# Two output projections of a two-block transformer kernel, each as seven block products in place of eight

## The reference

```python
merged = sigmoid(a_r) * y_r + sigmoid(a_f) * y_f      # 1024 tokens x 1024, two gated heads' outputs
x = x + merged @ w_out[l]                             # the output projection, 1024 x 1024
h2 = rmsnorm(x, g_ffn[l])                             # block 1 goes on to its feed-forward
```

## Time and profile before

| | |
|---|---|
| time, median of 3 runs | 3076.11 us (3071.45 to 3077.84) |
| time of the profiled execution | 3070.67 us |
| its span | 3068.9 us |
| busy: PE, DVE, ACT, POOL | 96%, 49%, 34%, 31% |
| projection of block 1, first matmul to first of the feed-forward | 830.04 to 928.15 us |
| projection of block 2, first matmul to the end of the span | 2967.86 to 3068.9 us |
| matmuls of one projection | 384 |

### The profile page before, as it was taken

The page is one execution under the profiler, slowest core; times in us unless marked ns, Lnnn a source line. Parts: engine busy times, 40 slices in busy tenths (PEclk is TensorE's granted clock), DMA queues, the critical chain, the costliest instruction groups (busy, mean ns, idle before and its releaser), DMA issues.

```text
span 3068.9 us, 38355 instructions
## 1 busy us (share of the span) xinstructions
PE 2937.8 (96%) x14282; PEld 2348.7 (77%) x14282; DVE 1510.8 (49%) x2003; ACT 1038.5 (34%) x1732; POOL 942.6 (31%) x725
## 2 busy tenths in 40 slices
PE   7989999999998999999998999999999999999998
PEld 6778776788786888887887766668788888788886
DVE  2573656311317665653436488850556566651133
ACT  3232555300114333321223366641444444530011
POOL 2424110344442000003446600013333443444444
PEclk8999999999999999999999999999999999999999
DMA  3111000211224222224113300013323322241132
GB/s 127 42 47 55 18 28 18 93 48 45 75 82 141 83 83 83 83 90 185 47 48 125 101 7 14 21 37 103 86 71 81 82 74 79 73 158 48 44 110 86
DMA packets 107446, 224.13 MB, mean 73 GB/s; under 512 B 14001, under 2 KB 27057, under 8 KB 106801
## 3 DMA queue, kind: packets, MB, share of 16 engines
q1 hardware_dynamic: 67680, 134.01, 14.4%
q10 hardware_dynamic: 39632, 88.26, 8.4%
HBM read 167.70 MB, written 41.94 MB: 68 GB/s over the span
## 4 chain that ended last, share of the span: by engine, by line
PE 77%; DVE 11%; ACT 5%; issue 3%; POOL 2%; DMA 2%; ACTq 1%; POOLq 0%; SPq 0%; DVEq 0%
PE ps L356 17%; PE ps L372 13%; PE ps L2046 12%; PE ps L317 12%; PE ps L2166 7%; PE ps L1085 3%; PE ps L1116 1%; PE ps L2370 1%; DMA raw<-in_stream_dram 1%; DVE mla_ptl L1049 1%; ACT ps L1025 1%; PE ps L1101 1%; POOL wl L3373 1%; DVE mla_nm L1058 1%; PE ps L1103 1%
## 5 line engine op out<-in xcount | busy, mean ns | idle before, releaser
L3371 POOL TENSOR_TENSOR wh<-raw,zeros 128x512 fp32r<-128x512 f32 x356 | 397.9, 1118 | 2091.0 <-PE ps L372 559.7
L3373 POOL TENSOR_TENSOR wl<-raw,wh 128x512 fp32r<-128x512 f32 x356 | 531.5, 1493 | 27.9
L372 PE MATMUL ps<-hth,wh 128*128 128x512 f32 x704 | 285.0, 405 | 2.1 <-DVE fox_vl L1298 2.1
L372 PE MATMUL ps<-hth,wl 128*128 128x512 f32 x704 | 278.9, 396 | 0.0
L372 PE MATMUL ps<-htl,wh 128*128 128x512 f32 x704 | 278.7, 396 | 0.0
L317 PE MATMUL ps<-wh,hth 128*128 128x512 f32 (+2 forms) x608 | 237.3, 390 | 12.8 <-POOL wl L3373 7.7
L317 PE MATMUL ps<-wl,hth 128*128 128x512 f32 (+2 forms) x608 | 234.0, 385 | 0.0
L317 PE MATMUL ps<-wh,htl 128*128 128x512 f32 (+2 forms) x608 | 233.7, 384 | 0.0
L356 PE MATMUL ps<-hth,wh 128*128 128x512 f32 x496 | 196.6, 396 | 0.4 <-issue 0.3
L356 PE MATMUL ps<-hth,wl 128*128 128x512 f32 x496 | 196.3, 396 | 0.0
L356 PE MATMUL ps<-htl,wh 128*128 128x512 f32 x496 | 196.2, 395 | 0.0
(11 more groups left out here) (495 smaller groups left out, 6819.1 us busy)
## 6 DMA issues: line engine op xcount, KB each, us to landing
raw<-in_stream_dram SPq DMA_DIRECT2D x356, 256.0 KB, 2.6
up_raw<-in_stream_dram SPq DMA_DIRECT2D x21, 1024.0 KB, 5.7
dil_stg<-dil_stg ACTq DMA_DIRECT2D x96, 128.0 KB, 2.4
ff_dram<-ff SPq DMA_DIRECT2D x20, 512.0 KB, 3.0
dil_sz<-vd_dram ACTq DMA_DIRECT2D x12, 512.0 KB, 4.4
heads_raw<-heads_dram ACTq DMA_DIRECT2D x8, 512.0 KB, 7.2
norm_x<-in_x_dram ACTq DMA_DIRECT2D x1, 4096.0 KB, 16.1
x_dram<-norm_x ACTq DMA_DIRECT2D x8, 512.0 KB, 3.1
```

The lines of the kernel that those rows point to most:

```text
L372: ins = nc.tensor.matmul(ps[:, bank + half, :], w[:, j, c:c + P], a[:, k, HALF * half:HALF * half + HALF], start=k == 0 and q == 0, stop=k ...
L3371: nc.gpsimd.tensor_tensor(wh[:, s, :], raw[:, s, :], zeros[:].to_broadcast([P, HALF]), ALU.add).then_inc(w_hi, 1)
L3373: nc.gpsimd.tensor_tensor(wl[:, s, :], raw[:, s, :], wh[:, s, :], ALU.subtract).then_inc(w_split, 1)
```

## The change

`M` is cut in two by two blocks: P (features 0 to 511, tokens 0 to 511), Q (features 512 to 1023, the same tokens), and R and S for tokens 512 to 1023. The weights are cut in the same way into E, F (features 0 to 511; left and right output columns) and G, H (features 512 to 1023). The result's four blocks are made from seven block products, with sums of blocks as their operands: `pe` = P E, `qg` = Q G, `s1w1`, `s2w2`, `s4f`, `s3w3` and `rw4`, where S1 = R + S, S3 = Q - S, S2 = S1 - Q, S4 = P - S2, w1 = H - G, w2 = F - w1, w4 = E - w2, w3 = F - H. A block product is four weight units times four token tiles times 3 matmuls, 48 in all; the projection has 7 x 48 = 336 matmuls where it had 384.

- `pe`, `qg` and `s4f` take their weights from the stream (12 units for a projection, where there were 16), and each unit now serves four token tiles. The weights of the other four products are sums of blocks: ACT loads E, F, G, H again from a copy at the stream's end, DVE makes the sums, ACT their high parts `Wh`, DVE their low parts `Wl`.
- DVE makes the sums of blocks of `M` in place, and their low parts (`norm_ml`).
- `early_loads` and `early_sum` load H and G and make w1 at the start of the merge, in the second slot of the gates' tile `sg`; ACT's gates of column 1 wait for that (`early_summed`).
- Token tiles 0 to 3 are complete with the fifth product, `s4f`; their norm, and in block 1 the transposes of tiles 0 to 3, now lie within `s3w3` and `rw4`. The last product, `rw4`, is made token tile by token tile, 9 matmuls each.

```diff
-    plain(w["w_out"][0], range(KT))
+    def out_units(a):
+        for ks, c in ((K1, 0), (K2, 0), (K1, 1)):
+            for k in ks:
+                unit(rows(a, k, HALF * c, HALF))
+    out_units(w["w_out"][0])
...
-U_A, U_FOX, U_MERGE, U_OUT, U_UP, U_DOWN, U_LAT, U_MLA, U_DIL = 24, 28, 48, 16, 8, 44, 16, len(AHEAD) + 7, 80
+U_A, U_FOX, U_MERGE, U_OUT, U_UP, U_DOWN, U_LAT, U_MLA, U_DIL = 24, 28, 48, 12, 8, 44, 16, len(AHEAD) + 7, 80
...
+                if late:
+                    self.Wh = sb(name + "_wh", [P, 4, HALF], F32R, scope)
+                    self.Wl = sb(name + "_wl", [P, 4, HALF], F32R, scope)
+                    self.Ml = sb(name + "_ml", [P, KT, S], F32R, scope)
+                    self.S1h = sb(name + "_s1h", [P, 4, HALF], F32R, scope)
+                    with ExitStack() as over:
+                        self.E = sb(name + "_e", [P, 4, HALF], F32, over)
...
+            def early_loads(self, act):
+                act.dma_start(self.norm.F[:], self.weights(K2, 1)).then_inc(self.early_in, 16)
+                for br in range(2):
+                    act.dma_start(self.merge.sg[:, br, 1, :].rearrange("p (a n) -> p a n", a=2), self.weights(K2[2 * br:2 * br + 2], 0)).then_inc(self.early_in, 16)
+            def early_sum(self, dve):
+                dve.wait_ge(self.early_in, 48)
+                for br in range(2):
+                    at = self.norm.F[:, 2 * br:2 * br + 2, :]
+                    self.v.did(nc.vector.tensor_tensor(at, at, self.merge.sg[:, br, 1, :].rearrange("p (a n) -> p a n", a=2), ALU.subtract), "w1" + "ab"[br])
+            def early_summed(self, act):
+                self.v.wait(act, "w1b")
 
...
+                def copy(out, x, step):
+                    a.did(nc.scalar.activation(out, x, ACT.Copy), step)
+                def high(w, x, j, product):
+                    if product:
+                        p.wait(act, f"{product}.u{j}" if j < 3 else f"{product}.3")
+                    copy(n.Wh[:, j, :], x[:, j, :], f"h{w}.{j}")
...
+                m.py.wait(act, "y0", last)
+                act.dma_start(n.X[:, 0:4, :], self.source[:, 0:4, :]).then_inc(self.x_in[0], 16)
+                m.v.wait(act, "m1", last)
+                act.dma_start(n.E[:], self.weights(K1, 1)).then_inc(self.f_in, 16)
+                n.load(act)
+                m.v.wait(act, "sum", last)
+                copy(hth[:, last, 0:HALF], m.M[:, last, 0:HALF], f"hi{last}")
+                for j in range(4):
+                    high("w1", n.F, j, None)
+                v.wait(act, "s1b")
+                copy(n.S1h[:], self.R, "s1h")
...
+                v.wait(dve, "s3b")
+                tt(self.Q, self.R, self.Q, "s2")
+                a.wait(dve, "s1h")
+                v.wait(dve, "s2")
+                tt(self.low(1), self.R, n.S1h[:], "s1l")
+                for j in range(4):
+                    low("w1", n.F, j)
+                dve.wait_ge(self.x_in[0], 16)
+                for t in range(4):
+                    add("pe", t)
+                tt(self.P, self.P, self.Q, "s4")
+                dve.wait_ge(self.f_in, 16)
+                v.wait(dve, "lw1.3")
+                tt(n.F[:], n.E[:], n.F[:], "w2")
+                a.wait(dve, "s2h")
+                v.wait(dve, "s4")
+                tt(self.low(2), self.Q, n.S2h[:], "s2l")
+                for t in range(4):
+                    v.wait(dve, f"pe.{t}")
+                    add("qg", t)
+                v.wait(dve, "w2")
+                low("w2", n.F, 0)
+                low("w2", n.F, 1)
+                a.wait(dve, "s3h")
+                tt(htl[:, 4:8, t2], self.S, hth[:, 4:8, t2], "s3l")
+                low("w2", n.F, 2)
+                low("w2", n.F, 3)
+                dve.wait_ge(self.e_in, 16)
+                tt(self.S, self.S, n.F[:], "w4")
...
+                def product(k, x, bank, begins, free, unit=None, w=None, tiles=range(4), ready=lambda j: None, after=lambda j: None):
+                    for j in range(4):
+                        ready(j)
+                        if w:
+                            v.wait(pe, f"l{w}.{j}")
+                            b = n.Wh[:, j, :], n.Wl[:, j, :]
+                        else:
+                            use_unit(pe, unit + j)
+                            b = wh[:, j % 2, :], wl[:, j % 2, :]
+                        for t in range(4):
+                            if j == 0:
+                                free(t)
+                            head, ins = tile(k, x, t, j, b, bank, begins, begins and j == 0, j == 3)
+                            if not w and t == 0:
+                                head.then_inc(begun, 1)
+                        if w and j < 3:
+                            p.did(ins, f"{k}.u{j}")
+                        after(j)
...
+                product("pe", hl(k1, t1), 0, True, lambda t: m.a.wait(pe, "g0", last) if t < 2 else m.v.wait(pe, "m0", last), unit=u0, ready=lambda j: v.wait(pe, f"lo{j}"))
+                product("qg", hl(k2, t1), 4, True, lambda t: m.a.wait(pe, "g1", last) if t < 2 else m.v.wait(pe, "m1", last), unit=u0 + 4,
+                        ready=lambda j: v.wait(pe, "loqb" if j == 3 else "loqa"))
+                v.wait(pe, "s1l")
+                product("s1w1", (n.S1h, self.low(1)), 0, True, lambda t: v.wait(pe, f"pe.{t}"), w="w1")
+                v.wait(pe, "s2l")
+                product("s2w2", (n.S2h, self.low(2)), 4, False, lambda t: v.wait(pe, f"qg.{t}"), w="w2")
+                v.wait(pe, "s4l")
+                product("s4f", (n.S1h, self.low(0)), 0, False, lambda t: v.wait(pe, f"s1w1.{t}"), unit=u0 + 8)
+                v.wait(pe, "s3l")
+                def transposes(t):
+                    if not n.final:
+                        n.transposes(pe, t, lambda bank: self.bank_free(pe, bank))
+                product("s3w3", hl(k2, t2), 4, False, lambda t: v.wait(pe, f"s2w2.{t}"), w="w3", after=lambda j: transposes(j - 1) if j else None)
+                weight = lambda j: (n.Wh[:, j, :], n.Wl[:, j, :])
+                v.wait(pe, "lw4.0")
+                for t in range(4):
+                    v.wait(pe, f"s3w3.{t}")
+                    tile("rw4", hl(k1, t2), t, 0, weight(0), 4, False, False, False)
+                transposes(3)
+                for t in range(4):
+                    for j in range(1, 4):
+                        if t == 0:
+                            v.wait(pe, f"lw4.{j}")
+                        tile("rw4", hl(k1, t2), t, j, weight(j), 4, False, False, j == 3)
```

More of the change, by code:

```diff
@@ new lines, in high @@
+            def high(self, act, t):
+                for h in range(2):
+                    self.p.wait(act, f"tr{t}.{h}")
+                    x = ps[:, self.bank(t, h), :].rearrange("p (k n) -> p k n", k=4)
+                    self.a.did(nc.scalar.activation(hth[:, 4 * h:4 * h + 4, P * t:P * t + P], x, ACT.Copy), f"hi{t}.{h}")
+                    if self.keeps and t >= 4:
+                        self.a.did(nc.scalar.activation(self.full[h][:, :, P * (t - 4):P * (t - 4) + P], x, ACT.Copy), f"full{t}.{h}")
@@ L480, in act @@
                         continue
[L481 to L489 removed]
+                    self.high(act, t)
                     if store:
@@ L1666, in store, with summed @@
+            def summed(self, act, t, last):
+                self.v.wait(act, (("qg.{}", "s4f.{}"), ("s3w3.{}", "rw4.{}"))[t // 4][last].format(t % 4))
             def store(self, act, t):
@@ new lines, in low, with add @@
+                def low(w, x, j):
+                    a.wait(dve, f"h{w}.{j}")
+                    tt(n.Wl[:, j, :], x[:, j, :], n.Wh[:, j, :], f"l{w}.{j}")
+                def add(k, t):
+                    bank, tile, c = dict(pe=(0, 0, 0), qg=(4, 0, 0), s1w1=(0, 4, 1), s2w2=(4, 0, 1), s4f=(0, 0, 1), s3w3=(4, 4, 1), rw4=(4, 4, 0))[k]
+                    p.wait(dve, f"{k}.{t}")
+                    at = n.X[:, tile + t, HALF * c:HALF * c + HALF]
+                    tt(at, at, ps[:, bank + t, :], f"{k}.{t}", ALU.add)
@@ new lines, in dve @@
+                for k in range(4):
+                    a.wait(dve, f"hi{k}")
+                    tt(htl[:, k, :], M[:, k, :], hth[:, k, :], f"lo{k}")
+                m.column(dve, KT - 2, 0, M[:, KT - 2, :])
+                m.v.wait(dve, "sum", KT - 2)
+                v.wait(dve, "lo3")
+                tt(M[:, 0:3, t2], M[:, 0:3, t2], M[:, 4:7, t2], "s1a", ALU.add)
+                v.wait(dve, "s1a")
+                tt(M[:, 4:7, t2], M[:, 4:7, t1], M[:, 4:7, t2], "s3a")
+                m.gated(dve, last, 1, M[:, last, :], 0)
@@ new lines, in dve @@
+                whole("s4f", 0)
+                whole("s4f", 1)
+                n.scaled(dve, 0)
+                whole("s4f", 2)
+                n.scaled(dve, 1)
+                whole("s4f", 3)
+                for j in range(3):
+                    low("w4", self.S, j)
+                    if j < 2:
+                        n.lows(dve, j)
+                        n.scaled(dve, 2 + j)
```

(21 more changed lines are left out.)

335 lines of the change are left out of this document (231 added, 104 removed).

## The result

| | before | after |
|---|---|---|
| median of the runs taken together (17 each) | 3072.6 us | 3079.5 us |
| profiled execution: span | 3068.9 us | 3076.2 us |
| mean granted clock of TensorE | 0.985 | 0.983 |
| first projection, first matmul to the feed-forward's first | 98.1 us | 99.6 us |
| second projection, first matmul to the span's end | 101.0 us | 107.2 us |

The ratio is 1.002 with an interval of 1.0013 to 1.0027: the changed kernel is about 7 us **slower**, where 2 us less was forecast. 3079.5 lies in the range, but on the other side of the kernel before. The forecast's base, the median of three runs (3076.1), was 3.5 us above the median of all 17.

A forecast was written before the change was run, and what follows sets the result against it. TensorE's matmuls were taken as the bound. Block 1 -4.4, block 2 -0.7, early sum +2.0 and clock +1.2 summed to -1.9 us, from 3076.1 to 3074 us; range 3057 to 3086.

The forecast's parts named there:

- -4.4: First projection up to the feed-forward's first matmul: forecast 93.7 us against 98.1, before the clock term.
- -0.7: Second projection to the span's end: forecast 100.3 us against 101.0, before the early sum and clock terms.
- Matmuls: Both projections: 48 fewer matmuls each at 0.2333 us, 11.2 us saved per projection, 22.4 in all.
- Splits: Streamed units, walked through POOL, DVE and TensorE in turns: TensorE loses 10.1 us in block 1, 11.8 in block 2.
- The clock: Slow matmuls behind the waits in both projections: bounds 0 and 1.4 us each, middle taken, +1.2 for both.
- Add wait: Block 1, after the last matmul of `s3w3`: TensorE waits some 1.8 us for DVE's sum of that bank.
- Transposes: Block 1: four transposes now inside the projection, some 0.85 us each, 3.4 in all.
- Block 1's end: Before the feed-forward: idle 1.50 and 1.90 us and slow matmuls go; a rival, chance 0.08, had this not mended, 3078.
- Block 2's early sum: Block 2's merge: TensorE waits 2.0 us at the gates of column 2, which need w1 made first.
- Tail: Block 2, from the last matmul to the span's end: 10.1 us against 11.5.
- Late loads: Rival, chance 0.20: unit loads slowed by the new stage's loads delay splits, 4.5 us more per projection, 3085.
- POOL keeps up: Rival, chance 0.34 wholly or by half: DVE's long pieces miss POOL's splits, 3057, or 3066 halfway.

The follow-up runs named there:

- lates: The changed kernel with block E, the gain and the residual's second half asked for later, behind ACT's roundings of S3 and S2: 3079.3 us, ratio to before 1.0018.
- reorder: The changed kernel with DVE's S4, low parts and w3 moved to where POOL has no unit due, residual's second half loaded later: 3065.9 us, ratio to before 0.9982.
- cand: reorder with S2, S1's low part and w2 in four pieces each, and the second projection's first blocks requested earlier: 3060.3 us, ratio to before 0.9962.
- narrow: The changed kernel with DVE's long two-input pieces cut to 16 columns, ACT copies standing in, result not valid: 3062.1 us, ratio to before 0.9966.
- xlate: The changed kernel with only the residual's second half asked for later, some 10 us: 3079.0 us, ratio to before 1.0021.

## Why the prediction was wrong

The mechanism was named: splits shut out by DVE in turns, worth about what 96 matmuls save. The signs of the two stages were not: +1.4 where -4.4 stood, and +6.2 where -0.7 stood. By its steps:

- **Matmuls, -22.4: right**, and a little more. The products with weights held in SBUF take 10.9 us for 48, where the forecast has 11.2.
- **Splits, 10.1 and 11.8: too small.** From the last matmul of one unit to the first of the next, less 0.233 us each, they lost 13.2 and 13.9 us. The walk had unit 1 in time (it lost 1.2) and placed 2.1 and 2.0 before units 4 and 7, where 3.4 stood before unit 6 and 0.8 before unit 4 (first projection); unit 3 lost 3.4, not 2.7. The walk gives roughly the size of such a loss, not its places.
- **The clock, +1.2 for both: this step failed.** "Bounds 0 and 1.4 for each projection" were taken from one stretch of 3 us with seven slow matmuls. In the changed kernel 20 and 27 matmuls fell into stretches at half clock and cost 3.9 and 5.3 us more than at full clock: 9.2 in all, eight more than forecast and over three times what the two upper bounds allowed. One short stretch behind one stall is no upper bound where a stage has four stalls: here two stretches stood in the first projection and three in the second, each 3.4 or 6.8 us long.
- **The second matmul of a streamed unit: no term.** At full clock it starts some 0.31 us behind the first instead of 0.233, 0.7 and 0.6 us a projection.
- **Add wait, 1.8: 0.7. Transposes, 3.4: right.** **Block 1's end: right**; its gain, and 1.1 us more in the feed-forward's first block (27.7 us instead of 28.8), were eaten ahead of it.
- **Block 2's early sum, +2.0: 1.3. Tail, 10.1: 9.6**, with halves 2.7 us apart as worked out.
- **Late loads (rival, 3085):** its rows came (loads of 5.4 and 6.9 us, POOL late by 2.0 and 1.0 us), its effect did not (lates). **POOL keeps up:** fell in this kernel, and is what reorder and cand approach by another order.

The books: with its half of the clock's 1.2 us the forecast had -3.8 for block 1 and -0.1 for block 2, and 5.2 and 6.3 us are missing. In block 1 they are +3.1 (splits), +3.3 (clock), +0.7 (second matmuls), -0.6 (weights held in SBUF) and -1.2 (add wait and transposes), 5.3; in block 2 +2.1, +4.7, +0.6, -0.9, -0.5 (tail) and +0.4 for a short wait for DVE's sum, 6.4. So the clock is the largest miss and the splits, 5.2 us over both, the second.

That 3079.5 lies between 3057 and 3086 is luck: the upper part of the range was priced for late loads, which did not cause this, and the base stood 3.5 us too high.

What made the splits long is what the prediction leaned on, DVE and POOL in turns: one POOL instruction takes 1.04 us in *narrow* and 2.35 in *lates*. The Trainium skill's "SBUF — State Buffer", Who interferes with whom, has it as a rule: a DVE instruction with two inputs in SBUF contends with a GpSimd instruction that reads SBUF; these rows agree, and DVE's four sums with an input in PSUM left POOL alone (2.47 us from 848.22 in the changed kernel, beside POOL's 1.04 and 1.29). Of the half clock the runs show that it goes when the long waits go (cand, narrow's first projection). The Trainium skill's "TensorE: Matmul & The Clock Gate", Part 1: The HAM clock gate, describes the half rate as the state that idleness brings back, and that much agrees; which of the waits brings it back stays open, as the last section shows.

## What to carry to other kernels

When a change halves the time in which a streamed operand is used up, as here from 5.6 to 2.8 us, its preparation can become the bound: lay the two-input SBUF work of DVE where no split is due before anything else, for order alone turned +0.2% into -0.2%, and pieces with an earlier request into -0.4%. Price a string of stalls with the clock behind each of them: in this kernel's one traced execution some 0.3 us at half clock for each one lost at the units' starts (9.2 us for 27). A late load is a cause only if moving it moves the wait.

## What was not expected of the hardware

- **The half clock depends on more than one wait's length.** In *reorder* both projections waited 3.28 us before unit 3; nothing behind it ran at half clock in the first, and 3.4 us did in the second (the windows below). Over the 26 projections of the changed kernel and the twelve others: with two or more waits of over 3 us there was a stretch at half clock in 8 of 8, with one in 7 of 10, with none in 2 of 8; this is a count, not a rule. A wait of 1.88 us at 892.46 in the changed kernel was followed by 3.4 us at half clock, a wait of 1.88 us before the same unit in *xlate* by none. So one execution's dips are not a constant of a kernel; what decides it within a stage stays open.

```profile
843.00:851.00 8.00, 6.92 (x28) 5.09 (x29) 8.00 (x9) 0.00 (x0) 5.79 (x6) 1.00 0.24 66
2973.00:2981.00 8.00, 7.19 (x24) 5.60 (x24) 8.00 (x9) 0.00 (x0) 5.83 (x5) 0.79 0.20 68
```

- **Matmuls whose weights lie in `norm_wh` and `norm_wl` start 0.227 us apart**, those of streamed units 0.233, in every projection looked at. The cause was not tried.
- **DVE's small sum over 128x4 elements was shut out too.** It takes 0.16 us in the changed kernel, and 1.01 in reorder, where POOL's high part was running from 3013.91 to 3014.95; it has one tensor input only. The kernel before shows the same with 128x8 elements, 1.24 us beside POOL's low part.

```profile
3013.97 1.01 DVE L496 TENSOR_SCALAR norm_base<-norm_ss 128x4 f32<-128x4 f32 x1
```
